# Retention's weighted values as products of high and low parts, with the PSUM banks of its stage taken from another start

## The reference

```
q, k, v, g = split(x @ w_in)          # 4 x 256, 4 x 256, 4 x 512, 4 x 512 columns
q, k = rope(q), rope(k) * 256**-0.5
s     = (q_i k_j) * decay(i - j)       # per head, lower triangle
out   = s @ v                          # "weighted values"
y     = silu(g) * group_norm(out) * gn_g
mix   = y @ w_o
```

## Time and profile before

| | |
|---|---|
| median of 3 runs | 2068.78 us (2067.94 to 2069.36) |
| the profiled execution, its own time | 2070.33 us |
| its span, first to last instruction | 2067.7 us |
| TensorE busy | 2049.2 us, 99% |
| VectorE, ScalarE, GpSimd busy | 1525.6 us, 1052.9 us, 168.1 us |
| mean granted TensorE clock | 0.998 of 2.4 GHz |
| HBM read | 374.87 MB, 182 GB/s over the span |

### The profile page before, as it was taken

One profiled execution on the slowest core, in us unless ns is written; L12 is line 12 of the kernel. 1 busy time (PEld: TensorE's weight loads), 2 busy tenths in 40 slices (PEclk: granted clock), 3 DMA queues, 4 the chain that ended last, 5 costly groups with the idle time before them and its releaser, 6 DMA issues.

```text
span 2067.7 us, 27322 instructions
## 1 busy us (share of the span) xinstructions
PE 2049.2 (99%) x11347; PEld 1768.4 (86%) x11347; DVE 1525.6 (74%) x1680; ACT 1052.9 (51%) x1236; POOL 168.1 (8%) x94
## 2 busy tenths in 40 slices
PE   8999999999999999999999999999999999999998
PEld 7998888899988888778888988888888888788887
DVE  6878899787978767666766787666876667567665
ACT  5574655456555555455433665334653444455432
POOL 2001121020112105000000000000000005000000
PEclk9999999999999999999999999999999999999999
DMA  8544555564455555555655555655366556455652
GB/s 278 174 136 168 183 196 187 182 197 143 143 187 199 185 180 192 174 183 183 204 194 181 180 184 185 218 186 149 143 200 207 190 184 211 144 185 182 212 195 102
DMA packets 244740, 377.68 MB, mean 183 GB/s; under 512 B 14101, under 2 KB 179210, under 8 KB 244618
## 3 DMA queue, kind: packets, MB, share of 16 engines
q1 hardware_dynamic: 244474, 375.42, 55.1%
q10 hardware_dynamic: 144, 0.52, 0.1%
HBM read 374.87 MB, written 1.05 MB: 182 GB/s over the span
## 4 chain that ended last, share of the span: by engine, by line
PE 94%; DVE 3%; ACT 1%; DVEq 1%; DMA 0%; issue 0%; SPq 0%
PE bank L738 48%; PE acc L738 44%; PE bank L736 2%; DVE slot_lo L2036 1%; DVEq L2031 1%; ACT slot_hi L1507 1%; PE acc L736 0%; DMA slot<-in_w_in 0%; DVE arena L2776 0%; DVE arena L2782 0%; DVE arena L2397 0%; ACT split L1524 0%; DVE arena L2350 0%; DVE arena L2436 0%; ACT arena L1502 0%
## 5 line engine op out<-in xcount | busy, mean ns | idle before, releaser
L2036 DVE TENSOR_TENSOR slot_lo<-slot,slot_hi 128x2048 fp32r<-128x2048 f32 (+1 forms) x343 | 788.8, 2307 | 266.8 <-ACT slot_hi L1507 265.8
L1507 ACT ACTIVATE slot_hi<-slot 128x2048 fp32r<-128x2048 f32 (+1 forms) x343 | 650.3, 1904 | 381.7 <-DMA slot<-in_mlp_w 312.7
L738 PE MATMUL acc<-slot_hi,split 128*128 128x512 f32 x2236 | 713.1, 392 | 4.7 <-DVE slot_lo L2036 3.0
L738 PE MATMUL bank<-split,slot_hi 128*128 128x512 f32 (+1 forms) x2524 | 572.1, 355 | 0.3 <-ACT arena L1502 0.3
L738 PEld LDWEIGHTS acc<-slot_hi,split 128*128 128x128 f32 x2236 | 421.0, 188 | 93.5 <-issue 5.7
L738 PEld LDWEIGHTS bank<-split,slot_hi 128*128 128x128 f32 x2524 | 437.7, 190 | 59.6 <-issue 2.0
L738 PE MATMUL acc<-slot_lo,split 128*128 128x512 f32 x1118 | 436.7, 391 | 0.0
L738 PE MATMUL bank<-split,slot_lo 128*128 128x256 f32 x2094 | 353.7, 282 | 0.0
L738 PEld LDWEIGHTS bank<-split,slot_lo 128*128 128x128 f32 x2094 | 309.5, 191 | 16.2
L738 PEld LDWEIGHTS acc<-slot_lo,split 128*128 128x128 f32 x1118 | 210.7, 188 | 41.0 <-issue 1.0
L738 PE MATMUL bank<-slot_hi,split 128*128 128x512 f32 (+1 forms) x804 | 219.0, 381 | 0.6 <-ACT split L1524 0.6
(11 more groups left out here) (245 smaller groups left out, 1509.6 us busy)
## 6 DMA issues: line engine op xcount, KB each, us to landing
slot<-in_mlp_w SPq DMA_DIRECT2D x128, 1024.0 KB, 5.1
slot<-in_ret_w_in SPq DMA_DIRECT2D x48, 1024.0 KB, 5.1
slot<-in_w_up SPq DMA_DIRECT2D x40, 1024.0 KB, 5.1
slot<-in_w_in SPq DMA_DIRECT2D x37, 1024.0 KB, 5.3
slot<-in_w_down SPq DMA_DIRECT2D x22, 1024.0 KB, 4.8
slot<-in_ret_w_o SPq DMA_DIRECT2D x16, 1024.0 KB, 4.9
slot<-in_lru_w_in SPq DMA_DIRECT2D x10, 1024.0 KB, 5.2
slot<-in_w_out SPq DMA_DIRECT2D x8, 1024.0 KB, 4.9
```

Of the source, the lines that this page charges most:

```text
L738: i = nc.tensor.matmul(o, w, m, start=start, stop=stop)
L1507: A(whi[u.r][:, 0:u.cols], raw[u.r][:, 0:u.cols], ACT.Copy).then_inc(slot_hi[u.r], 1)
L2036: TTO(wlo[u.r][:, 0:u.cols], raw[u.r][:, 0:u.cols], f32(whi[u.r][:, 0:u.cols]), ALU.subtract)\
```

## The change

In both retention stages the weighted values become three fp32r products each. The high part of the values is ScalarE's copy itself, now written as fp32r (`rvs[0]`, same place as `rv`); the low part is made by VectorE in the 4096 columns of `split1` (`low_values`), which now also is what frees the value banks. The high part of the decayed scores is a new ScalarE copy (`rds[0]`), the low part a new VectorE subtraction (`low_decayed`), in pairs: head h's low part follows head h+1's multiplication by the decay table. `low_values(8)`, for the first value chunk, stands ahead of the rotations; the other three stand behind the odd chunks 11, 13, 15. Semaphores `rv_hi`, `rsd_ready`, `rsd_hi`, `rsd_lo` tie this together. In `plan()` the ring over eight banks starts at bank 4 in both stages, where it started at 7 in the first and at 0 in the second.

```
--- before.py
+++ after.py
@@ -248,7 +248,7 @@
     def retention(n):
         k = f"r{n}"
         head("ln5" if n else "x0", k + "w", (8, 9), k + "w", [(8, tt) for tt in range(TT)])
-        banks.use(NBANK, None, 0 if n else NBANK - 1)
+        banks.use(NBANK, None, NSUM)
         if n == 0:
             bank("par", [1])
         for c in range(8):
@@ -370,7 +370,9 @@
         stat = sb("stat", 1024)
         posi, posf = trig[:, 0, :].bitcast(I32), trig[:, 1, :]
         prows = trig[:, 2:4, :].rearrange("p a s -> p (a s)").rearrange("p (l a n) -> p l a n", l=DEPTH, a=2)
+        arena_at = -(-nc.sbuf_base // 32) * 32
         arena = sb("arena", 17408)
+        rounded = nc.alloc_sbuf_tensor_at("rounded", [P, 17408], F32R, offset=arena_at)
         bank = [ctx.enter_context(nc.psum_tensor(f"bank{r}", [P, 512], F32)) for r in range(NSUM)]
         acc = ctx.enter_context(nc.psum_tensor("acc", [P, TT, D], F32))
         bank += [acc[:, tt, h * 512:(h + 1) * 512] for tt in range(TT) for h in range(HALVES)]
@@ -424,6 +426,8 @@
         rv = area(6144, TT, 2048)
         rg = area(10240, TT, 2048)
         rsd = area(14336, RH, MAP)
+        rds = [rounded[:, at:at + RH * MAP].rearrange("p (h n) -> p h n", n=MAP) for at in (4096, 14336)]
+        rvs = [a.rearrange("p (t n) -> p t n", n=2048) for a in (rounded[:, 6144:10240], spl[1][:, :])]
         rsum = [area(10240 + 1024 * i, 2, 512) for i in range(2)]
         rin = [area(12288 + 512 * i, 2, S) for i in range(2)]
 
@@ -475,7 +479,7 @@
         slot_free = [sem(f"slot_free{r}") for r in range(NSLOT)]
         bank_full = [sem(f"bank_full{r}") for r in range(NBANK)]
         bank_read = [sem(f"bank_read{r}") for r in range(NBANK)]
-        names = ("rot_summed rot_ready ident_loaded first_loaded first_hi first_lo loaded gain_loaded pos_loaded x_loaded0 x_loaded1 rows_loaded grows_loaded tok_loaded zeroed angles_ready softplus_in softplus_exp lam_in lam_exp "
+        names = ("rv_hi rsd_ready rsd_hi rsd_lo rot_summed rot_ready ident_loaded first_loaded first_hi first_lo loaded gain_loaded pos_loaded x_loaded0 x_loaded1 rows_loaded grows_loaded tok_loaded zeroed angles_ready softplus_in softplus_exp lam_in lam_exp "
                  "x_squared var_ready std_ready xn_ready qk_squared qk_var qk_std c_scaled roped_ab roped_c "
                  "scores_max probs probs_scaled diff_ready yc_var yc_std yc_ready branches_added merge_added merged acc_full x_ready x_halves "
                  "conv_scaled conv_done silu_done hid_ready hid_used relu_done rot_out gn_var gn_std ro_gated "
@@ -1228,10 +1232,14 @@
                     transposes(banks[k + "t", i], ro, 2 * i)
 
                 for h in range(RH):
-                    in_sbuf(k + "s", [h])
+                    wait(V["rsd_lo"], 4 * n + h + 1)
                     for tt in range(TT):
                         o, end = open_bank(banks[k + "o", 2 * h + tt])
-                        weighted(o[:, :], rsd[:, h, :], lambda kt: rv[:, kt, h * RDV:(h + 1) * RDV], tt, end)
+                        for kt in range(tt + 1):
+                            c = (tt + kt) * P
+                            product(o[:, :], lambda i: rds[i][:, h, c:c + P],
+                                    lambda i: rvs[i][:, kt, h * RDV:(h + 1) * RDV], kt == 0, kt == tt,
+                                    end if kt == tt else None)
                     if h == 3:
                         for i in range(2):
                             turned(i)
@@ -1816,7 +1824,9 @@
                 k = f"r{n}"
                 def values(c):
                     for tt in range(TT):
-                        copies(k + "w", (c, tt), rv[:, tt:tt + 1, (c - 8) * 256:(c - 6) * 256])
+                        u = banks[k + "w", (c, tt)]
+                        full(act, u)
+                        A(rvs[0][:, tt, (c - 8) * 256:(c - 6) * 256], bank[u.r][:, :], ACT.Copy).then_inc(V["rv_hi"], 1)
 
                 for c in (8, 9):
                     weights.ahead(slots[k + "w", c])
@@ -1846,6 +1856,9 @@
                                  scale=parg[:, G_RET + 16 * n + f:G_RET + 16 * n + f + 1])
                     last.then_inc(V["hi_out"], 1)
 
+                for h in range(RH):
+                    act.wait_ge(V["rsd_ready"], 4 * n + h + 1)
+                    A(rds[0][:, h, :], rsd[:, h, :], ACT.Copy).then_inc(V["rsd_hi"], 1)
                 for h in range(RH):
                     weights.ahead(slots[k + "w", 16 + 2 * h])
                     act.wait_ge(V["gn_var"], 4 * n + h + 1)
@@ -2647,6 +2660,16 @@
                     T(parg[:, :], bank[u.r][:, 0:G_ALL]).then_inc(bank_read[u.r], 1)
                     d()
                     dve.wait_ge(V["trig_ready"], 1)
+                def low_values(c):
+
+                    for tt in range(TT):
+                        u = banks[k + "w", (c, tt)]
+                        cs = slice((c - 8) * 256, (c - 6) * 256)
+                        dve.wait_ge(V["rv_hi"], 8 * n + c - 8 + tt + 1)
+                        TTO(rvs[1][:, tt, cs], bank[u.r][:, :], f32(rvs[0][:, tt, cs]), ALU.subtract)\
+                            .then_inc(bank_read[u.r], 1)
+
+                low_values(8)
                 for c in range(8):
                     weights.ahead(slots[k + "w", c])
                     rotated(c, 8 * n + c, cosr, sinr, n0, n0 + c)
@@ -2654,12 +2677,28 @@
                     weights.ahead(slots[k + "w", c])
                     if n == 0 and c == 10:
                         softplus()
+                    if c % 2:
+                        low_values(c - 1)
                 dve.wait_ge(V["tab_full"], tabs[k + "decay", 0].fills)
-                for h in range(RH):
+
+                def decayed(h):
+
                     b = banks[k + "s", h]
                     full(dve, b)
                     TTO(rsd[:, h, :], bank[b.r][:, 0:MAP], tab[:, h * MAP:(h + 1) * MAP], ALU.mult)\
                         .then_inc(bank_read[b.r], 1)
+                    dve.drain().then_inc(V["rsd_ready"], 1)
+
+                def low_decayed(h):
+
+                    dve.wait_ge(V["rsd_hi"], 4 * n + h + 1)
+                    TTO(rds[1][:, h, :], rsd[:, h, :], f32(rds[0][:, h, :]), ALU.subtract).then_inc(V["rsd_lo"], 1)
+
+                decayed(0)
+                for h in range(1, RH):
+                    decayed(h)
+                    low_decayed(h - 1)
+                low_decayed(3)
                 dve.drain().then_inc(V["tab_free"], 1)
                 def low(i):
 
```

## The result

The changed kernel takes 2079.26 us (median of 4 runs, 2078.72 to 2079.68) against 2069.07 us (4 runs, 2067.94 to 2069.73). The ratio is 1.0049, 95% interval 1.0037 to 1.0061: slower by 0.5%, 10.2 us. The prediction was 2079.1 us, 2075.0 to 2082.8. The profiled execution has a span of 2077.4 us against 2067.7, 9.7 us more.

What follows compares the result with a forecast made beforehand. TensorE, busy 99% of the span, bounds the kernel. Waits of 4.7 and 5.4 us less 6 x 0.54 saved give +6.9, the clock +3.4, together +10.3: 2079.1 us for the median, 8 in 10 range 2075.0 to 2082.8.

Steps and rivals of the forecast that it cites:

- the clock's term: TensorE's clock falls behind both new waits ahead of gate chunk 22: 1.7 us each, 3.4 us in all.
- The wait: Gate chunk 22 waits for head 3's banks, starting 4.7 us later in the first stage, 5.4 us in the second.
- The step on what ends it: VectorE's normalizing of head 3 ends the waits; cheaper matmuls don't bring it forward; chunk 22 starts at 905.35 and 1829.2.
- The products: Weighted values: nine products at 0.227 us replace three float32 matmuls, 2.04 us against 2.58, saving 0.54 us a head.
- my upper bound: Clock's cost at one new wait at most 3.4 us, if the low stretch were two of the earlier trace's 3.42 us.
- The work at nothing: Added VectorE work (15 us) and ScalarE copies (8 at 0.50 us) fit into spare time and cost nothing.
- The scores' chain: Head 0's low part of the decayed scores ready at 855.4, wanted by TensorE at 856.36: margin 0.9 us, taken at 0.
- (1): Rival: the waits ahead of gate chunk 22 come but the clock doesn't charge: +6.9, 2075.7 us; chance 0.22.
- (3): Rival: the waits for the last head's banks don't bind, eight heads save 4.3 us: 2064.5 us; not slower, 0.06.
- (2): Rival: clock stays low longer or the scores' chain misses its margin: +13 to +15, 2082 to 2084 us; chance 0.10.
- (4): Rival: products run slower, for instance 0.25 us a step: +11.5, 2080.3 us; counted within the forecast's chance of 0.62.

Runs made afterwards that it cites:

- e2: The kernel before with only the ring's start moved to bank 4 in both stages, weighted values left in float32: 2082.31 us, ratio 1.0066.
- e1: The changed kernel with the eight-bank ring starting at bank 5 in the first retention stage and 6 in the second: 2064.98 us, ratio 0.9979.
- e5: The changed kernel with 44 transposes into an unread bank ahead of gate chunk 22 in both stages: 2075.31 us, ratio 1.0031.
- e8: The changed kernel with the ring from 5 and 6 and the first value chunk's low parts behind the first rotation, first stage only: 2064.18 us, ratio 0.9975.
- e3: The changed kernel with 20 fp32r matmuls into an unread bank ahead of gate chunk 22 in both stages: 2076.25 us, ratio 1.0034.
- e4: The changed kernel with the ring's old starts, bank 7 in the first stage and 0 in the second: 2070.17 us, ratio 1.0006.
- e7: The changed kernel with the ring from 5 and 6 and the first value chunk's low parts behind the first rotation, both stages: 2071.23 us, ratio 1.0010.
- e6: The changed kernel with the ring from bank 5 in the first stage, still from 4 in the second: 2073.22 us, ratio 1.0017.

## Why the prediction was right

Its direction, its size and its mechanism held. That the number fits to 0.2 us is luck: the clock's term was 1.3 us too small, and the RG-LRU stage happened to give 1.7 us back.

**The wait.** Read off the ring's order and the timeline as 4.7 and 5.4 us for the start of gate chunk 22, its price alone. e2, which has only this, shows waits of 4.5 and 5.2 us. The pauses were forecast as 5.3 and 6.0 us; they are 5.01 and 5.73 in the list, which counts from the end of the last transpose, and 5.2 and 6.0 counted as the forecast did, from where gate chunk 22 would have started. The step on what ends it held too: VectorE's chain hangs on ScalarE's work behind gate chunk 20, and head 3's own saving does not bring it forward. It starts to normalize 1.5 us earlier in the first stage, which is what heads 0 to 2 save, but 7.21 us behind the start of head 3's weighted values in both kernels (897.26 to 904.47, 895.74 to 902.95).

**The products.** 0.54 us a head was forecast, with a step of 0.227. The step is 0.232 (2.09 us for nine), so 0.50 us. e1 gives 4.0 us for all eight heads where 4.3 were forecast. By the four passes of the Trainium skill, page "FP8 and Floating Point Precision", section "TensorE Precision Notes", it would have been 5.4 us; nearer is the row.

**The clock.** The size was off. I took one low stretch of 3.42 us for each wait, 3.4 us in all. The two stretches of work at half clock are 4.0 and 5.4 us, 4.7 us in all; the low stretches were two of those of rows 9 each, the length of my upper bound, and part of them fell into the waits. The sum was met because the low stretch at the RG-LRU stage, 1.7 us, was missing in the profiled execution of the changed kernel: 4.7 - 1.7 = 3.0. I had counted that stretch as a fixed part of the kernel; the traced runs and the groups in e5 and e8 say that it comes and goes. With it the change would have cost 11.9 us, still inside the range.

**The work at nothing.** It held: e1 has all of it and no wait. The scores' chain, with 0.9 us of margin by my count, holds (timeline of the changed kernel, VectorE and TensorE, beside the earlier trace rows):

```profile
853.04 0.56 DVE L2688 TENSOR_TENSOR arena<-bank,tab 128x384 f32<-128x384 f32 x1
854.98 0.56 DVE L2695 TENSOR_TENSOR rounded<-arena,rounded 128x384 fp32r<-128x384 f32 x1
856.62 0.47 PE L742 MATMUL acc<-rounded 128*128 128x512 f32 x1
```

Head 0's low part ends at 855.54 and TensorE takes it at 856.62. VectorE's statistics of head 0 came at 862.11, 2.3 us later than before (2.5 by my estimate), and nobody waited.

**The rivals.** (1) falls with e3: filling the pause gives 3 us back, so the clock does charge. (3), that head 3's banks don't bind, falls with e2. But its time, 2064.5, is what the products give once the order is mended: e1 and e8 measured 2065.0 and 2064.2. Half of (2) came true: the clock stayed low longer than in rows 9, at a cost 1.3 us above the forecast. Its other half, the scores' chain, did not, and the time stayed below its 2082. (4) has the step at 0.25; it is 0.232.

## What to carry to other kernels

Where a ring hands out buffers, a change of its start, width or order is a change of who waits for whom: write down for each buffer the last user before and after, above all where the ring narrows or restarts, and look up in the trace when that user reads it. A bound engine that pauses for some microseconds pays twice, for the pause and for the low clock behind it, so price a new wait by its length and by a low stretch of the same trace, and leave room to twice that stretch: here it was missed by 1.3 us in 3.4. When one change carries a gain and a shift in order, run each alone: here the gain was 4 us and the shift cost 13 to 14.

## What the runs showed of the hardware that was not expected

- The same 2.6 us wait at the RG-LRU stage, behind the same work, is followed by a granted clock of 0.50 in the profiled run of the kernel before and by 1.00 in that of the changed kernel. Of the ten traced kernels six show the fall (before, e1, e3, e4, e5, e7) and four do not (changed, e2, e6, e8). It is worth 1.7 us, nearly 0.1%. The 22 runs of the kernel before beside e1 fall in two groups of 11, with spans of 2065.8 to 2066.4 and 2067.3 to 2068.2 us and mean clocks of 0.999 and mostly 0.998; that the fall is what parts them rests on that and on the traced runs of e5 and e8, one of either group.
- The fall need not come in the pause. In e2, behind a wait of 4.5 us, gate chunk 22 starts at full pace (0.47 us for its first matmul at 905.18, 0.77 at the low clock), and the clock is at 0.50 from 905.71 on.
- The stretch of work at the low clock was 4.0 and 5.4 us behind the changed kernel's waits of 5.0 and 5.7 us, 5.4 us behind the 3.55 us wait of e4 and 5.8 us behind the 4.65 us wait of e7, but 3.4 and 4.3 us behind e2's waits of 4.5 and 5.2 us, and 3.4 us behind the 2.6 us wait of the earlier trace rows: a wait's length does not tell it.
- 44 float32 transposes in a row kept the clock at 2.4 GHz in both stages (1.00 in the windows of e5).
- A float32 matmul of 512 columns costs 0.86 us from start to start (2.58 us for three), three fp32r products of the same size 0.70 (2.09 us for nine): three passes on high and low parts are the faster form, if the parts are made beside other work.
